# The front of a hybrid attention and state-space block on one Trainium2 core: a new order of its projection units, convolution taps in PSUM, later folds and value turns, earlier right-hand sums

## The reference

```python
u = rms_norm(h, norm_w)                                  # h: 16 meta tokens, then 2048 frames, width 1024
q, k, v, sb_gate, ssd_z, xbc, dt_raw = split_cols(u @ w_in)
o_sb = stick_breaking_attention(q, k, v)                 # 16 heads of 64
y_sb = rms_norm(o_sb * silu(sb_gate), sb_norm_w)
xbc = silu(causal_depthwise_conv(xbc, conv_w, conv_b))   # 1536 columns, 4 taps
o_ssd = ssd_chunked(xs, softplus(dt_raw + dt_bias), a, bmat, cmat, d_skip)
y_ssd = rms_norm(o_ssd * silu(ssd_z), ssd_norm_w)
h = rms_norm(h + concat(y_sb, y_ssd) @ w_out, final_norm_w)[:, 16:]
```

## Time and profile before

| | us |
|---|---|
| median of 3 runs | 2860.26 (2857.64 to 2861.21) |
| the profiled execution | 2855.09 |
| its span, first to last instruction | 2853.4 |
| `front_stage`, first to last product | 58.01 to 1242.50 |

### The profile page before, as it was taken

How to read it: one execution, slowest core, us unless ns; L and a number is a source line. 1 busy time by engine, 2 the same in 40 slices (tenths; PEclk the granted TensorE clock), 3 DMA queues, 4 the chain that set the end, 5 groups by cost and what they waited for, 6 DMA issues and landing times. The chain is left out here.

```text
span 2853.4 us, 41550 instructions
## 1 busy us (share of the span) xinstructions
PE 2635.4 (92%) x14314; PEld 1852.2 (65%) x14314; DVE 1845.6 (65%) x2097; ACT 1325.6 (46%) x2095; POOL 1680.0 (59%) x1270
## 2 busy tenths in 40 slices
PE   4799998897999988979998999999999999599998
PEld 3577886675888866756665555555555555378887
DVE  4643218946331179429997888988988889655554
ACT  2433432234434332321117777877778787422221
POOL 3887776668888767747865666655666556100000
PEclk8899999998999999989998999999999999899999
DMA  2254332121553322224462112122121212242231
GB/s 92 90 173 165 108 117 78 74 90 60 177 169 109 106 89 85 93 68 129 129 180 87 53 57 85 60 60 75 38 83 60 60 31 71 86 147 88 88 103 45
DMA packets 202408, 267.99 MB, mean 94 GB/s; under 512 B 12833, under 2 KB 136033, under 8 KB 195569
## 3 DMA queue, kind: packets, MB, share of 16 engines
q1 hardware_dynamic: 202224, 265.64, 28.9%
HBM read 168.84 MB, written 96.76 MB: 93 GB/s over the span
## 5 line engine op out<-in xcount | busy, mean ns | idle before, releaser
L1842 POOL TENSOR_TENSOR a_w<-a_beta,a_rest 128x1024 f32<-128x1024 f32 (+2 forms) x320 | 560.8, 1753 | 352.9 <-DVE a_rest L1799 207.1
L755 POOL TENSOR_TENSOR f_l_lo<-f_wst,f_l_hi 128x512 fp32r<-128x512 f32 x312 | 422.7, 1356 | 265.0 <-ACT f_l_hi L654 264.9
L1799 DVE TENSOR_TENSOR_SCAN a_rest<-a_keep,a_rest,a_ones 128x513 f32<-128x513 f32 x384 | 469.9, 1261 | 10.8 <-ACT a_keep L1769 10.8
L1719 PE MATMUL a_turn<-a_ident,a_w 128*128 128x128 f32 (+1 forms) x2432 | 342.7, 279 | 7.3 <-DVE a_wt L1753 6.1
L1734 PE MATMUL a_o<-a_wt,a_v 128*64 128x512 f32 (+3 forms) x1408 | 338.5, 559 | 8.9 <-DVE a_out L1809 8.9
L1753 ACT COPY a_wt<-a_turn 128x512 f32<-128x512 f32 (+3 forms) x440 | 225.3, 529 | 205.2 <-PE a_turn L1719 203.7
L1719 PEld LDWEIGHTS a_turn<-a_ident,a_w 128*128 128x128 f32 (+1 forms) x2432 | 256.5, 140 | 91.5 <-issue 66.1
L558 PE MATMUL f_y<-f_t_hi,f_l_hi 128*128 128x512 f32 x624 | 259.0, 415 | 48.6 <-DVE f_u L998 24.2
L1769 ACT ACTIVATE a_keep<-a_z 128x1024 f32<-128x1024 f32 (+4 forms) x352 | 299.8, 852 | 4.6 <-PE a_z L1702 4.5
L1769 ACT ACTIVATE a_beta<-a_z 128x1024 f32<-128x1024 f32 (+4 forms) x352 | 299.6, 851 | 0.0
L558 PE MATMUL f_y<-f_t_lo,f_l_hi 128*128 128x512 f32 x624 | 251.5, 403 | 0.0
(11 more groups left out here) (220 smaller groups left out, 5167.5 us busy)
## 6 DMA issues: line engine op xcount, KB each, us to landing
f_wst<-in_w_pairs SPq DMA_DIRECT2D x52, 1024.0 KB, 5.4
scratch_gate<-f_out SPq DMA_DIRECT2D x64, 256.0 KB, 2.5
o_g<-scratch_mixed SPq DMA_DIRECT2D x32, 512.0 KB, 5.5
s_xc<-scratch_xbc SPq DMA_DIRECT2D x16, 768.0 KB, 5.3
scratch_xbc<-f_out SPq DMA_DIRECT2D x36, 256.0 KB, 2.1
scratch_q_hi<-f_out SPq DMA_DIRECT2D x32, 256.0 KB, 2.9
scratch_q_lo<-f_out SPq DMA_DIRECT2D x32, 256.0 KB, 3.7
scratch_v<-f_out SPq DMA_DIRECT2D x32, 256.0 KB, 2.3
```

The lines of the kernel that those rows point to most:

```text
L755: return nc.gpsimd.tensor_tensor(out, a, b, op).then_inc(done, 1)
L1719: mm = nc.tensor.transpose(turn[h][0:rows, qi * P:(qi + 1) * P], tile[:, h, x:x + rows], ident[:, :])
L1799: mm = nc.vector.tensor_tensor_scan(rest[r % RS][:, h, tn - 1::-1], top, ones[:, 0:1].to_broadcast([P, tn]), start, ALU.mult, ALU.min)
L1842: nc.gpsimd.tensor_tensor(w[r % AS][:, :, 0:tn], beta[r % KEEPS][:, :, 0:tn], rest[r % RS][:, :, 1:tn + 1], ALU.mult).then_inc(w_ready, 1)
```

## The change

The units get another order: `q q q q`, six gates, then `k conv k conv v conv k conv v conv k conv v gate v gate`, the same in both passes. The weights in memory stay as they are (`PAIR_AT`).

The taps of the convolution write PSUM: `conv_acc` are the two banks of `f_pt`, by turns; the sixteen meta columns have taps of their own into `f_lead_acc`. `convolve` does two taps a tick, from tick 4 of the unit to tick 11, that is tick 4 of the next unit. ACT's silu reads the bank and writes `f_out`; ACT, not DVE, copies c = 0 to `f_row` (`conv_first`). v results go to tiles of the ring `f_out` ("raw") in place of `f_row`.

q becomes `f_q4`, made by DVE from `f_p1` and the bank at i = 1; ACT's copy of product 1 and POOL's sum are gone. The norm tiles stand in units 1 to 8, their dt part after i = 6 and the fold after i = 0 of the next unit; the fold of the meta columns is after i = 4; values are turned a product later (`FINISH`).

For pass two the sum of operand 1 goes to the free `f_row` tiles and is made in unit 23, that of operand 4 in unit 24; those of 2 and 6 stay in unit 25, at i = 1 and i = 4. The low part of operand 5 is POOL's.

```diff
+    KIND = ["q"] * 4 + ["gate"] * 6 + ["k", "conv", "k", "conv", "v", "conv", "k", "conv", "v", "conv", "k", "conv",
+                                       "v", "gate", "v", "gate"]
-        if 4 <= n < 4 + NT // 2:
+        if NORM_FROM <= n < NORM_FROM + NT // 2:          # NORM_FROM = 1
             SIDE[n] = "norm"
+    FINISH = {"k": {3: 0, 4: 3, 5: 1, 6: 2}, "q": {3: 0, 4: 3, 5: 1, 6: 2}, "gate": {3: 0, 4: 3, 5: 1, 6: 2},
+              "conv": {6: 0, 8: 1, 10: 2, 12: 3}, "v": {5: 0, 6: 3, 7: 1, 8: 2}}
+        lead_acc = m_.psum("f_lead_acc", [P, W])
+        conv_acc = [pt[:, 4 * b:4 * (b + 1), :].rearrange("p q f -> p (q f)") for b in range(2)]
+        def right_source(p, i, k):
+            if p and i == 1:
+                return rows[:, k * W:(k + 1) * W]
...
                 if i == 5:
-                    pe.wait_ge(p5_ready, START + n + 1)
+                    pe.wait_ge(q_ready, START + n + 1)
...
-                if i == 2:
-                    pool.wait_ge(p1_ready, START + n + 1)
-                    pool.wait_ge(p5_ready, START + n + 1)
-                    add(p5[:, :], p1[:, :], p5[:, :], ALU.add, q_ready)
+                if n == UNITS - 3 and i == 5:
+                    right_sums(1, 1)
+                if n == UNITS - 2 and i == 3:
+                    right_sums(1, 4)
                 if n == UNITS - 1:
-                    right_sums(1, (1, 2, 4, 6, None, None, None)[i])
+                    if i == 1:
+                        right_sums(1, 2)
+                    if i == 4:
+                        right_sums(1, 6)
+                    if i == BY_POOL:                       # 5
+                        right_low(i)
...
+            def convolve(n, c, part):
+                acc = conv_acc[turn % 2]
+                if part == 0:
+                    if turn >= 2:
+                        dve.wait_ge(act_out, finished(n, CONV_ORDER[turn - 2]))
+                    if meta_here(n, c % 2):
+                        for tap in range(CONV):
+                            tap_step(lead_acc[:, 0:META], here[:, first:first + META], blk, tap)
+                for tap in (0, 1) if part == 0 else (2, 3):
+                    tap_step(acc, here[:, at + tap:at + tap + W], blk, tap)
...
+                if i == 1 and n < N:
+                    nc.vector.tensor_tensor(q4[:, :], p1[:, :], bank_z[:, :], ALU.add).then_inc(q_ready, 1)
+                for x in range(max(0, n - 1), min(N, n + 1)):
+                    step = m - PRODUCTS * x - CONV_FIRST
+                    if kind(x) == "conv" and 0 <= step < 2 * len(CONV_ORDER):
+                        convolve(x, CONV_ORDER[step // 2], step % 2)
-                if n == UNITS - 1:
+                if n == UNITS - 1 and i != BY_POOL:
                     right_low(1, i)
```

## The result

The kernel after took **2776.2 us** (median of 4 runs, 2772.9 to 2777.8), the kernel before 2860.7 beside it: a ratio of 0.9705 with an interval of 0.9688 to 0.9722. The forecast was 2778, in a range of 2763 to 2812.

What follows compares the result with a forecast made beforehand. PE, 92% busy, bounds the kernel but waits in the front, in conv stretches for DVE's sums delayed by slow taps. Excess falls from 158.9 to 78.8 us, saving 80.1, plus 2 at the start: 2860.3 - 82 = 2778, range 2763 to 2812.

Steps and rivals of the forecast that it cites:

- Taps into PSUM: Convolution taps: 0.75 us each writing PSUM, so 12.0 us a conv unit against 17.6 (pass one) and 19.0.
- Conv stretches at PE's own work: Conv units and the unit behind each: no waits left, only side products (1.77 each) and value turns (1.87 a v unit).
- The term of 0.5 us on each of six conv units: Pass one: allowance for DVE's backlog of 4 to 5 us from tiny copies and sixteen-column taps; 3 us in all.
- the 2 us for ACT's fourth table load: Unit after conv: a fourth table load on ACT, and DVE's second softplus step may hold c22; 2 us put on it.
- The load by product: DVE's work per product in pass two: backlog peaks near 1.5 us and is made up, so no wait is left.
- the formula: Conv units: PE loses 16t + 8 - 24.5 us each with taps of t us, nothing until t = 1.03.
- taps collide: Rival: PSUM taps still collide with POOL; 2810 at 1.2 us, 2899 at 1.66; chance 0.08 (1.0 to 1.4 us), slower 0.03.
- Norm tiles: Units with norm tiles: 2.0 us each for all 8, where the four in q units cost 3.4; q norm units at 21.0.
- q off ACT and POOL: One DVE sum of 0.69 us replaces ACT's copy and POOL's sum; gives nothing by itself, makes room on POOL.
- The turn of the passes: Units 25 and 26: 16 to 24 us over their floor, 18 taken, in place of 30.6.
- The left tile after the second batch is ready 0.8 us early: POOL's moved sums: the left tile after the second batch is ready 0.8 us before PE wants it.
- The start, -2 us: Unit 0: POOL's sums can begin where 1.89 us of idle time began, as q comes first; 2 us saved.

Runs made afterwards that it cites:

- e1_taps_sbuf: The kernel after with the taps summing in SBUF tiles again in place of PSUM, order of after kept: 2821.7 us, ratio 0.9871.
- e2_psum_alone: The kernel before with only the taps moved into PSUM, order of units and place of taps as before: 2796.6 us, ratio 0.9783.
- e7_q_on_pool: The kernel after with q made as before, by ACT's copy of product 1 and POOL's sum: 2778.3 us, ratio 0.9719.
- e4_low5_dve: The kernel after with the low part of right-hand operand 5 back on DVE: 2774.6 us, ratio 0.9703.
- e9_all_three: The kernel after with sums ahead of the first left tile, DVE's low parts of the turn later, and both early sum batches at their units' first product: 2765.5 us.
- e5_start_first: The kernel after with ACT's first high parts and POOL's operand 1 sums ahead of the first left tile: 2770.0 us, ratio 0.9686.

## Why the prediction was right, and where not

By its own steps, from the trace of after:

- **Taps into PSUM: right.** 756 ns at the median for the price of 0.75, never in POOL's way. The argument that an input in PSUM keeps clear of POOL was thinner than it read: of the 52 `f_u` named for it only 10 ran beside a POOL operation (673 to 682 ns). The 73 taps that ran wholly beside POOL in after are the better proof. 48 first taps at 808 ns were priced at 0.75, and 48 lead taps at 0.24 to 0.29 for 0.16; 3 + 5 us of DVE's time in all, none on PE's path. On the first taps the Trainium skill (VectorE: DVE Perf Modes, "The perf-mode tier table") was right: the estimate from it was 0.27 us more than the form into SBUF, whose fastest took 532 ns in e1_taps_sbuf, and 808 - 532 is 0.28.
- **Conv stretches at PE's own work: right**, to 0.5 us in 253, with clock 1.00. The term of 0.5 us on each of six conv units and the 2 us for ACT's fourth table load were both nothing (unit 22 and the units behind conv lie on their floors, 3 + 2 us too much). The load by product was counted well, and its limit too strictly, by the same 2 us as the formula.
- **Why it works: right, but the shares were not told apart.** The prediction priced the conv stretches only with both edits at once. e2_psum_alone shows that the tap's price alone carries 62 of 84 us, and that the alternation then adds 6. The new order with the norm tiles and the turn, but without it, carries 37 (e1_taps_sbuf). The rival "taps collide" came up in that kernel alone.
- **Norm tiles: right**, 21.04 for 21.0, and PE has no wait for `f_half` any more.
- **q off ACT and POOL: right**, nothing by itself (e7_q_on_pool).
- **The turn of the passes: 23.6 over in place of 18**, inside the 16 to 24 given. The end of the last low part was as worked out (666.94, T + 49, in T + 45 to 53). The sign given for it, "units 25 and 26 together near 57", was missed by 4.6. The step that failed is "then q and u and three products". `f_u` was done at T + 50.1, and three products behind it would be T + 58.3. But product 4 started at T + 53.5, since product 3 had waited for a left tile behind POOL's low parts and then ran at a lower granted clock (0.54, 4.94 us for 2.72). The sum had put four operations into POOL's queue and counted only what they spare DVE; that POOL could be the chain stood only among the rivals. e4_low5_dve shows the net: nothing.
- **"The left tile after the second batch is ready 0.8 us early": wrong.** The batch was as long as put (5.04 us), but ACT's next `f_l_hi` waited 4.81 us for what is behind it, and with it DVE's first low part came 1 us later than before (T + 6.2 for T + 5.2). Price on PE: 0.9 us (e9_all_three).
- **The start, -2 us: there for four products, then mostly lost.** Unit 0 ends at 113.06, 0.4 later than before, but the front also began 1.0 later. Counted from its first instruction, POOL's first sum comes 1.6 us earlier (8.07 for 9.68), near the 1.9 read off in the earlier trace rows, and product 4 starts 1.8 us earlier (52.75 for 54.53), so the chain named was the right one. Then products 4 and 5 take 8.31 us for 7.15, at granted clocks of 0.50 and 0.91 for 0.61 and 1.00, and only 0.6 is left at unit 1 (63.78 for 64.40). The prediction had no term for the clock there. In e4_low5_dve, with the same start, the two products run at 0.66 and 1.00 and the gain is 1.9. Why the clock differs is open. What could still be won lay ahead of that chain, in POOL's wait for the first weights: e5_start_first gains 5.2 there.

The sum over 19.04 a unit beside unit 0 is 79.3 in the trace and 78.8 in the prediction. That closeness is partly luck: 5.6 too little at the turn and 5 too much for small waits. Of the time of the profiled execution 2.4 us went missing at the start (1.0 of them because the front began later) and 1.8 us behind the front; the medians then lay 7.2 us further apart than the profiled executions. So that 2776.2 lies so near to 2778 is luck as well.

## What to carry to other kernels

Ask first whether an engine is late because it has too much to do or because its instructions run at a multiple of their best time: a spread of 750 to 1828 ns on one line is worth more than any reordering, and here one change of an output's place removed it. When work is moved to another engine's queue, price what stands behind it there, and look at the left-hand and right-hand side of that queue as one: a batch of four at the wrong place was worth as much as it saved. Put the short results that the bound engine waits for ahead of bulk work on each in-order queue; it gave 3.4 us at the turn and needs no new buffer. And before a few us at the head of a stage are put down to an edit, count from the stage's first instruction: the stage ahead, with the same code, ended up to 3.4 us earlier or later from one execution to the next.

## What the runs showed of the hardware

- Accumulating in PSUM from DVE costs within 1% of what it does in SBUF without POOL beside it: 756 ns at the median for a 128x512 tap that reads one SBUF and one PSUM input and writes PSUM, each waiting for the one before, against 751 for the 39 taps of e1_taps_sbuf that no POOL operation overlapped.
- Beside a POOL operation the same tap in SBUF took 1069 to 1842 ns (65 cases), in PSUM 743 to 757 (73 cases).
- The collision with POOL hits small and one-input instructions as well: in e1_taps_sbuf the sixteen-column lead taps with two inputs run from 234 to 1343 ns, and the first taps (one SBUF tensor input) take 532 to 543 with no POOL operation beside them and 1086 to 1561 wholly beside one, 1649 at worst. With the output in PSUM their maxima are 240 and 816.
- POOL is held up too: its sums run at 1.26 us in the batch of 612.74 (5.04 for four), where DVE does no low parts, and its operations at 1.5 to 1.7 beside them (5.91 and 6.76 for four).
